# Four transposes of the probabilities ahead of the next unit's scores, in the attention of the second block's latents

## The chip, the cores and the metric

The kernel runs on one core of one Trainium2 chip. The metric is the device time of one execution in microseconds (us), as the median of several runs. Engines are named as the profile names them: PE (TensorE matmul), PEld (TensorE weight load, which overlaps PE), DVE (VectorE), ACT (ScalarE), POOL (GpSimd) and SP (the queue of transfers).

## What is computed

Two transformer blocks on 512 tokens ("latents") of width 1024. The change lies in the second block, which has two layers. Each layer has a differential attention of 8 heads, in which the 512 latents attend to 768 keys (their own 512 and 256 of a context). Cut to what matters:

```
def diff_attention(q, k, v, lam):
    s = jnp.einsum('bqahd,bkahd->bahqk', q, k).astype(jnp.float32) * (B_QK_DIM ** -0.5)
    p = jax.nn.softmax(s, axis=-1)
    a = (p[:, 0] - lam * p[:, 1]).astype(v.dtype)
    return jnp.einsum('bhqk,bkhe->bqhe', a, v)
```

Every head has two queries and two keys of 64 features (index `a`). Two softmaxes over the same 768 keys are made, the second is subtracted with a factor, and the difference weighs the values, which are 128 wide. Around it stand projections of 1024 columns and more, a spatial gate, a gated convolution, and three gated branches (`a`, `c`, `b`), each a large product.

## The kernel before

The program is a list of steps, `order`. Each engine walks the whole list and emits its own instructions of each step, so that the order of work on an engine is the order of the list, and no engine overtakes itself. A part (`DiffAttention`, `HeadNorm`, `Branch`, `Gemm`) has methods `tensor`, `scalar` and `vector` for PE, ACT and DVE. Semaphores tie the engines together.

`DiffAttention` works in units: unit u is one head and 128 of the 512 queries, 32 units in a layer. Each of its even steps, number 2t, is what I call block t on PE:

- the scores of unit t (L1592): four matmuls, of 512 and then of 256 keys for each of the two `a`, into PSUM banks 2 and 3 and banks 4 and 5. Each has 64 rows, the two `a` lie on different halves of the array, and the profile shows each of them as two matmuls, x8 in all;
- the first four transposes of unit t-1 (L1572, `turn(pe, t - 1, 0)`), four 128x128 pieces of its probabilities `p0` into bank 7;
- the product of unit t-2 with the values (L1604), 6 matmuls, x12 in the profile;
- the last two transposes of unit t-1 (`turn(pe, t - 1, 1)`), into bank 7 again.

Around it, for one unit: DVE takes the maximum of each of the two score matrices (L1649) and turns it into a bias (L1653). ACT makes the two exponentials and their sums (L1623); ahead of them it copies the first four transposes of the unit before out of bank 7, and behind them the last two (L1632, `pT`). DVE then folds the two probabilities into one, `p0` (L1660, L1662, L1665, semaphore `diff_folded`, in the code `self.pn`), and scales and clips the product of the unit two before (L1672, L1675). The scores of the next unit go to the same banks as those just folded, so that PE waits for `diff_folded` before it begins them; the transposes read `p0` and wait for the same. `turn(..., 0)` waits besides for ACT's copy of the last two transposes of the unit before that (`diff_probsT`, in the code `self.pt`), `turn(..., 1)` for that of the first four.

Between two blocks the program puts other products of PE, the filler: pieces of the branches `a` and `c` and of the convolution, made of full-width matmuls of 512 columns (L365 to L367), in portions of 12, 24 or 36. `spread_between` mixes them by their sizes, with the steps of `HeadNorm` (transposes L1718, ACT L1731 and L1736, DVE L1756). No part of that planning looks at what a block contains, and the change leaves it as it is. Weights come through a ring of five slabs (SP transfers, POOL splits them in two parts).

Of the kernel before, what the change touches and what calls it, by code (L numbers as in the profile page):

```python
# [89 lines left out]
def program(nc, rows, w, ada_in, x_in, xc_in, mem_in, cc_in, cols_in, cst_in, rel_in, onehot_in, toe_mask_in, lam_in,  # L90
            rope_in, tri_in, flip_in, sgu_in, out):
    with ExitStack() as ctx:
# [53 lines left out]
        def pb(bank, n, o=0):  # L146
            return ps[:, 512 * bank + o:512 * bank + o + n]
# [57 lines left out]
        def tile_out(tile, n, o=0):  # L205
            return pb(tile_bank[tile], n, o)
# [71 lines left out]
        class Part:  # L278
# [11 lines left out]
            def tensor(self, pe, i):  # L290
                pass
# [57 lines left out]
        def bank_ready(pe, tile):  # L349
            if tile_nth[tile]:  # L350
                pe.wait_ge(tile_free[tile_bank[tile]], tile_nth[tile])
# [1168 lines left out]
        class DiffAttention(Part):  # L1520
# [54 lines left out]
            def tensor(self, pe, i):  # L1575
                if i % 2:
                    return
                t = i // 2
                if t == 0:
                    for c in self.clear:  # L1580
                        pe.wait_ge(*c())
                if t < self.N:
                    h, b = self.units[t]
                    if b == 0:
                        for c in self.ready_kv(h):
                            pe.wait_ge(*c)
                    if t:
                        pe.wait_ge(self.pn, self.pn0 + t)
                    for n0, n1 in ((0, 512), (512, TT)):
                        for a in range(2):  # L1590
                            r = slice(HD * a, HD * a + HD)
                            mm = nc.tensor.matmul(pb(2 + 2 * a, n1 - n0, n0), self.q[r, h, b * P:(b + 1) * P],  # L1592
                                                  self.k[r, h, n0:n1], start=True, stop=True)
                            if n1 == TT:
                                mm.then_inc(self.s, 1)
                if 0 <= t - 1 < self.N:
                    self.turn(pe, t - 1, 0)
                u = t - 2
                if 0 <= u < self.N:
                    h, b = self.units[u]  # L1600
                    pe.wait_ge(self.pt, self.pt0 + 2 * u + 2)
                    bank_ready(pe, self.tile[u])
                    for b in range(TT // P):
                        mm = nc.tensor.matmul(tile_out(self.tile[u], P), self.pT[u % 2][:, b * P:(b + 1) * P],  # L1604
                                              self.v_[:, b, h * P:(h + 1) * P], start=(b == 0), stop=(b == TT // P - 1))
                    mm.then_inc(tile_done, 1)
                if 0 <= t - 1 < self.N:
                    self.turn(pe, t - 1, 1)
# [1320 lines left out]
```

## Time and profile before

| | |
|---|---|
| median of 3 runs | 3592.96 us |
| lowest and highest | 3591.21 and 3599.41 us |
| the profiled execution's own time | 3596.96 us |
| its span in the trace | 3594.1 us |
| mean granted clock of PE | 0.977 |
| scores of the latents' attention, first and last start | 1719.6 and 3046.9 us |

The profiled execution is 4.0 us above the median. The two attentions take the stretches from about 1720 to 2020 us (layer 0) and from 2758 to 3060 us (layer 1). A start in the trace is when the instruction began; a matmul's duration holds its way through the array, so that the steps from start to start tell how much of PE it takes.

### The profile page before, as it was taken

Reading aid. Unit: us, or ns where it says so; the run is one execution under the profiler, and the core shown is the slowest. Engines: PE = TensorE matmul, PEld = TensorE weight load, DVE = VectorE, ACT = ScalarE, POOL = GpSimd, SP = SyncE. Lnnn points to the kernel's source line nnn. Section 1 sums busy time; section 2 is a strip of 40 time slices with the busy share of each in tenths; the row PEclk is TensorE's granted clock in tenths of the full one; section 3 lists DMA queues with packets and bytes.
Section 4 is the critical chain, followed back from the end, with each engine's and each line's share of the span. In section 5 each row is a group of like instructions: output and inputs, shape, how many; then the busy total and the mean of one; then the engine's idle time right before and its main releaser. Section 6 shows DMA issues by size and latency. Waiting matters only on the chain. (4 is left out here: it accounts for less than half of the span.)

```text
span 3594.1 us, 50262 instructions
## 1 busy us (share of the span) xinstructions
PE 3451.7 (96%) x19738; PEld 2922.5 (81%) x19738; DVE 1489.2 (41%) x3064; ACT 1032.0 (29%) x2793; POOL 2029.4 (56%) x1216
## 2 busy tenths in 40 slices
PE   7999989999999999899999999999999999999999
PEld 6877777877789988899777788888898777888887
DVE  7833641244873221452455314441343555134320
ACT  2146443133102110342344313220232444112210
POOL 4465363654569988746433456665564342656655
PEclk9999999989999999899999999999999999999999
DMA  7533122222664433332111222322222111223222
GB/s 288 202 137 111 62 97 106 85 87 106 222 223 146 147 130 117 136 116 87 65 59 48 77 94 89 100 93 95 107 91 78 64 53 47 95 88 100 94 90 98
DMA packets 109883, 388.91 MB, mean 108 GB/s; under 512 B 12057, under 2 KB 16537, under 8 KB 108242
## 3 DMA queue, kind: packets, MB, share of 16 engines
q1 hardware_dynamic: 89280, 315.10, 25.3%
q10 hardware_dynamic: 20370, 70.61, 5.6%
q8 instruction: 158, 2.59, 0.3%
q14 instruction: 75, 0.61, 0.1%
HBM read 379.34 MB, written 6.32 MB: 107 GB/s over the span
## 5 line engine op out<-in xcount | busy, mean ns | idle before, releaser
L2726 POOL CAST whi<-raw 128x1024 fp32r<-128x1024 f32 (+1 forms) x606 | 620.8, 1024 | 1504.0 <-DMA raw<-in_w 1503.4
L2728 POOL TENSOR_TENSOR wlo<-raw,whi 128x1024 fp32r<-128x1024 f32 (+1 forms) x606 | 1423.2, 2349 | 48.5
L365 PE MATMUL ps<-hhi,whi 128*128 128x512 f32 x1688 | 670.5, 397 | 19.6 <-DVE q L1675 8.5
L367 PE MATMUL ps<-hhi,wlo 128*128 128x512 f32 x1688 | 663.1, 393 | 0.0
L366 PE MATMUL ps<-hlo,whi 128*128 128x512 f32 x1688 | 661.5, 392 | 0.0
L365 PEld LDWEIGHTS ps<-hhi,whi 128*128 128x128 f32 x1688 | 318.5, 189 | 90.0 <-DVE q L1675 9.4
L367 PEld LDWEIGHTS ps<-hhi,wlo 128*128 128x128 f32 x1688 | 318.2, 189 | 71.9
L366 PEld LDWEIGHTS ps<-hlo,whi 128*128 128x128 f32 x1688 | 318.6, 189 | 66.7
L589 PE MATMUL ps<-whi,hhi 128*128 128x256 f32 (+1 forms) x960 | 276.8, 288 | 0.0
L591 PE MATMUL ps<-whi,hlo 128*128 128x256 f32 (+1 forms) x960 | 270.7, 282 | 0.0
L590 PE MATMUL ps<-wlo,hhi 128*128 128x256 f32 (+1 forms) x960 | 270.6, 282 | 0.0
L365 PE MATMUL ps<-chi,whi 128*128 128x256 f32 x656 | 190.8, 291 | 0.1
L366 PE MATMUL ps<-clo,whi 128*128 128x256 f32 x656 | 187.8, 286 | 0.0
L367 PE MATMUL ps<-chi,wlo 128*128 128x256 f32 x656 | 187.5, 286 | 0.0
L590 PEld LDWEIGHTS ps<-wlo,hhi 128*128 128x128 f32 x960 | 184.4, 192 | 0.1
L591 PEld LDWEIGHTS ps<-whi,hlo 128*128 128x128 f32 x960 | 184.4, 192 | 0.0
L589 PEld LDWEIGHTS ps<-whi,hhi 128*128 128x128 f32 x960 | 184.0, 192 | 0.1
L1649 DVE TENSOR_REDUCE small_d<-ps 128x1 f32<-128x768 f32 x128 | 121.8, 951 | 127.5 <-PE ps L1592 127.5
L837 DVE SCALAR_TENSOR_TENSOR f_sum<-ps,cols,f_sum 128x511 f32<-128x511 f32 x88 | 65.9, 749 | 239.6 <-ACT f_sum L882 239.6
L882 ACT ACTIVATE f_sum<-ps,cols 128x512 f32<-128x512 f32 x88 | 68.4, 779 | 269.3 <-PE ps L367 259.9
L365 PE MATMUL ps<-f_hi,whi 128*128 128x512 f32 x352 | 138.3, 393 | 0.0
L366 PE MATMUL ps<-f_lo,whi 128*128 128x512 f32 x352 | 137.6, 391 | 0.0
(427 smaller groups left out, 7029.7 us busy)
## 6 DMA issues: line engine op xcount, KB each, us to landing
raw<-in_w SPq DMA_DIRECT2D x574, 512.0 KB, 3.3
ada<-in_ada ACTq DMA_DIRECT2D x96, 512.0 KB, 4.7
raw<-in_w SPq DMA_DIRECT2D x16, 384.0 KB, 3.2
att_toe<-toe_dram ACTq DMA_DIRECT2D x12, 256.0 KB, 3.3
raw<-in_w SPq DMA_DIRECT2D x16, 192.0 KB, 2.4
x<-in_x SPq DMA_DIRECT2D x4, 512.0 KB, 9.6
cond<-in_cc ACTq DMA_DIRECT2D x2, 1024.0 KB, 7.2
kc_dram<-kc ACTq DMA_DIRECT2D x2, 1024.0 KB, 4.9
```

What stands on the lines that cost most here:

```text
L365: nc.tensor.matmul(o, whi[:, buf, c], hi[:, k, 0:n], start=(k == 0), stop=False)
L366: nc.tensor.matmul(o, whi[:, buf, c], lo[:, k, 0:n], start=False, stop=False)
L367: mm = nc.tensor.matmul(o, wlo[:, buf, c], hi[:, k, 0:n], start=False, stop=(k == kt - 1))
L589: nc.tensor.matmul(o, self.hi[:, k, a], whi[:, s % RING, c], start=(k == 0), stop=False)
L590: nc.tensor.matmul(o, self.hi[:, k, a], wlo[:, s % RING, c], start=False, stop=False)
L591: mm = nc.tensor.matmul(o, self.lo[:, k, a], whi[:, s % RING, c], start=False, stop=(k == KT - 1))
L837: return nc.vector.scalar_tensor_tensor(dst[:, 1:n], src[:, 0:n - 1], w0, dst[:, 1:n], ALU.mult, ALU.add)
L882: nc.scalar.activation(self.sum(m), self.out(m), ACT.Identity, bias=cols[:, b:b + 1], scale=cols[:, w1:w1 + 1]).then_inc(self.mid, 1)
L1649: nc.vector.tensor_reduce(small[0][:, a:a + 1], pb(2 + 2 * a, TT), AX_X, ALU.max)\
L2726: nc.gpsimd.tensor_copy(whi[:, buf, 0:c], raw[:, buf, 0:c]).then_inc(slab_hi, 1)
L2728: nc.gpsimd.tensor_tensor(wlo[:, buf, 0:c], raw[:, buf, 0:c], whi[:, buf, 0:c].bitcast(F32), ALU.subtract).then_inc(slab_split, 1)
```

## The change

The wait for `diff_folded` and the first four transposes of unit t-1 stand ahead of the scores of unit t. Block 32, which has no scores, has its transposes where it had them. Nothing is added or removed but one of two waits for the same count.

```diff
                     if t:
-                        pe.wait_ge(self.pn, self.pn0 + t)
+                        self.turn(pe, t - 1, 0)
                     for n0, n1 in ((0, 512), (512, TT)):
                         for a in range(2):
 ...
                             if n1 == TT:
                                 mm.then_inc(self.s, 1)
-                if 0 <= t - 1 < self.N:
+                if t == self.N:
                     self.turn(pe, t - 1, 0)
                 u = t - 2
```

The orders of DVE, ACT, POOL and SP are the same as before. On PE, block 1 of layer 0, the first with transposes and the only one with transposes and no product (the rows above it are filler, `k`, `q` and `cst`, `diff_p` are scores and transposes; numbers behind names count tensors):

```order
 L367 MATMUL ps<-hhi,wlo 128x512
-L1592 MATMUL ps<-k_170,q_169 128x512 [waits diff_folded]
-L1592 MATMUL ps<-k_170,q_169 128x512
-L1592 MATMUL ps<-k_170,q_169 128x256 x2
 L1572 MATMUL ps<-cst,diff_p_191 128x128 [waits diff_folded]
 L1572 MATMUL ps<-cst,diff_p_191 128x128 x3
+L1592 MATMUL ps<-k_170,q_169 128x512 x2
+L1592 MATMUL ps<-k_170,q_169 128x256 x2
 L1572 MATMUL ps<-cst,diff_p_191 128x128 [waits diff_probsT]
 L1572 MATMUL ps<-cst,diff_p_191 128x128
```

The scores now stand between the first four transposes and the last two. On PE, block 3 of the same layer, one like nearly all others (`v` marks the product of unit 1 with the values):

```order
 L366 MATMUL ps<-ab_lo,whi 128x512
 L367 MATMUL ps<-ab_hi,wlo 128x512
-L1592 MATMUL ps<-k_170,q_169 128x512 [waits diff_folded]
-L1592 MATMUL ps<-k_170,q_169 128x512
-L1592 MATMUL ps<-k_170,q_169 128x256 x2
 L1572 MATMUL ps<-cst,diff_p_191 128x128 [waits diff_probsT,diff_folded]
 L1572 MATMUL ps<-cst,diff_p_191 128x128 x3
+L1592 MATMUL ps<-k_170,q_169 128x512 x2
+L1592 MATMUL ps<-k_170,q_169 128x256 x2
 L1604 MATMUL ps<-v_171,diff_p_194 128x128 [waits tile_free6,diff_probsT]
```

The transposes moved from between scores and product to ahead of the scores, and took the wait with them.

## Rows read from the trace of the kernel before

**Rows 1.** The page's part 1: busy time, share of the span, instructions

```profile
PE 3451.7 (96%) x19738; PEld 2922.5 (81%) x19738; DVE 1489.2 (41%) x3064; ACT 1032.0 (29%) x2793; POOL 2029.4 (56%) x1216
```

**Rows 2.** Waits of PE, 1715 to 2030 us: us in total, times, longest

```profile
PE ps L365 <- DVE q L1675: 4.3, 1, 4.3
```

**Rows 3.** Waits of the weight loads (PEld), the same stretch

```profile
PEld ps L1592 <- DVE diff_p L1665: 8.4, 10, 3.0
...
PEld ps L1572 <- DVE diff_p L1665: 0.4, 1, 0.4
```

**Rows 4.** Timeline of PE, block 3: start, duration, what, count

```profile
1744.58 0.39 PE L366 MATMUL ps<-ab_lo,whi 128*128 128x512 f32 x1
1744.81 0.40 PE L367 MATMUL ps<-ab_hi,wlo 128*128 128x512 f32 x1
1745.21 1.56 PE L1592 MATMUL ps<-k,q 64*128 64x512 f32 x8
1746.70 0.66 PE L1572 MATMUL ps<-cst,diff_p 128*128 128x128 f32 x4
1747.19 1.50 PE L1604 MATMUL ps<-v,diff_p 128*128 128x128 f32 x12
1748.54 0.38 PE L1572 MATMUL ps<-cst,diff_p 128*128 128x128 f32 x2
```

**Rows 5.** Timeline of DVE, blocks 2 and 3

```profile
1744.14 1.02 DVE L1665 SCALAR_TENSOR_TENSOR diff_p<-ps,small_d,diff_p 128x768 f32<-128x768 f32 x1
...
1746.85 0.96 DVE L1649 TENSOR_REDUCE small_d<-ps 128x1 f32<-128x768 f32 x1 [0.50 <-PE ps L1592]
1747.84 0.15 DVE L1653 TENSOR_SCALAR small_d<-small_d 128x1 f32<-128x1 f32 x1
...
1750.62 1.02 DVE L1665 SCALAR_TENSOR_TENSOR diff_p<-ps,small_d,diff_p 128x768 f32<-128x768 f32 x1
```

**Rows 6.** Timeline of ACT, block 3

```profile
1747.46 0.60 ACT L1632 ACTIVATE diff_p<-ps 128x512 f32<-128x512 f32 x1 [3.59 <-PE ps L1572]
1748.03 0.90 ACT L1623 ACTIVATE diff_p<-ps,small_d 128x768 f32<-128x768 f32 x1
...
1749.97 0.37 ACT L1632 ACTIVATE diff_p<-ps 128x256 f32<-128x256 f32 x1
```

**Rows 7.** Timeline of PE, filler to scores at block 2

```profile
1738.41 0.40 PE L367 MATMUL ps<-hhi,wlo 128*128 128x512 f32 x1
1738.73 0.70 PE L1592 MATMUL ps<-k,q 64*128 64x512 f32 x2
```

**Rows 8.** Timeline of PE, filler to transposes, behind the attention of layer 0

```profile
2049.04 0.39 PE L367 MATMUL ps<-hhi,wlo 128*128 128x512 f32 x1
2049.27 0.49 PE L1718 MATMUL ps<-cst,q 128*128 128x128 f32 x3
```

**Rows 9.** Timeline of PE in the context's attention: transposes, scores, product

```profile
385.49 0.44 PE L1835 MATMUL ps<-cst,c_p 128*128 128x128 f32 x2
385.86 0.70 PE L1812 MATMUL ps<-kc,qc 64*128 64x256 f32 x2
386.49 0.71 PE L1847 MATMUL ps<-vc,c_p 128*128 128x128 f32 x4
387.03 0.59 PE L1282 MATMUL ps<-att_toe,att_flip 128*128 128x512 f32 x1
```

**Rows 10.** Timeline of PE, block 1

```profile
1727.27 1.56 PE L1592 MATMUL ps<-k,q 64*128 64x512 f32 x8 [0.37 <-DVE diff_p L1665]
...
1730.11 0.44 PE L1572 MATMUL ps<-cst,diff_p 128*128 128x128 f32 x2 [0.69 <-ACT diff_p L1632]
```

**Rows 11.** Timeline of DVE, block 21, and block 30 with the filler behind it

```profile
1908.85 0.95 DVE L1649 TENSOR_REDUCE small_d<-ps 128x1 f32<-128x768 f32 x1
...
1996.50 0.70 DVE L1075 SCALAR_TENSOR_TENSOR ps<-G,ps 128x512 f32<-128x512 f32 x1 [3.19 <-PE ps L367]
```

**Rows 12.** Timeline of PE, block 26 of layer 0

```profile
1950.99 2.93 PE L1592 MATMUL ps<-k,q 64*128 64x512 f32 x8 [2.77 <-DVE diff_p L1665]
```

## The prediction

> **What bounds the kernel now.** I read the page's busy shares first. PE is busy for 96% of the span and no other engine for more than 56% [rows 1], so the time is PE's stream of instructions plus its idle time; a change of PE's order can only move the idle time and what it costs to go from one kind of matmul to the next. Then PE's waits in the attention of layer 0. The matmuls idle 4.3 us for a clipped product once [rows 2] and 0.7 us for a copy once [rows 10]. For the fold I read the weight loads' waits, since they show short ones too: 8.4 us at 10 of the 31 blocks whose scores have to wait for it [rows 3], found by going through the starts of the scores and the ends of the fold. These are blocks 1, 3, 6, 11, 13, 14, 22, 26, 29 and 30. Block 8, with 0.14 us between fold and scores, belongs to them; and block 32 (no scores, four transposes first) waits for the fold already, the one time in [rows 3]. Layer 1 has the same blocks in the same state. I call them tight, the others loose: there the fold had ended 0.5 us or more before the scores began.
>
> **The loop that binds a tight block.** Block 3: the fold of unit 2 ends at 1744.14 + 1.02 = 1745.16 and the scores start 0.05 later [rows 4, 5]. DVE idles 0.50 us for them, so nothing of its own holds the maximum up. It starts 1.64 us after the scores' start, and the fold of unit 3 ends at 1751.64: 6.43 us from the start of the scores to the end of the fold. With the 0.05 this makes a loop of 6.48 us. PE's work in the same loop, with the smallest portion of filler, is about 6.40 us. The two limits are nearly equal, and what is put between the fold and the scores lengthens the first.
>
> **What the four transposes cost there.** They take 1747.19 - 1746.70 = 0.49 us from start to start when they stand behind scores, and I take the same when they stand behind an idle PE (in both cases the first waits for its weights). Going over to 64-row scores costs more: in the context's attention two transposes and the way to the scores take 0.37 us [rows 9], against 0.22 for two at 0.11 (12 matmuls of the same size take 1.35 [rows 4]) and 0.05 that the first is late behind scores. That leaves 0.10 for the way. So the scores of a tight block start 0.05 + 0.49 + 0.10 = 0.64 us after the fold instead of 0.05: the loop becomes 7.07 us, **+0.59 us**.
>
> **Does the earlier turn shorten that loop?** This is what could pay it back: ACT copies the first four transposes just ahead of its exponentials. The copy ended at 1748.06 and the exponential started at 1748.03 [rows 6], the bias it needs was there at 1747.84 + 0.15 = 1747.99 [rows 5]. The copy cost 0.04 us, and the second exponential does not feel it: it waits for the second maximum. I put the gain at 0; at most 0.04. The new wait in front of the scores, for the copy of the last two transposes, ends at 1750.34, 1.3 us before the fold [rows 5, 6]: it costs nothing, since ACT makes that copy right behind the exponentials for which the fold waits too.
>
> **Loose blocks.** The order goes from filler, scores, transposes, product to filler, transposes, scores, product. Filler to scores takes 0.32 us [rows 7] where a step of filler takes 0.23 [rows 4], and filler to transposes takes 0.23 [rows 8]: -0.09. Transposes that don't follow scores take 0.44 and not 0.49: -0.05. The way from transposes to scores is new: +0.10. The way from scores to whatever follows is paid as before, but the product now pays for following it: four matmuls took 386.49 to 387.03 = 0.54 [rows 9], against 0.45: +0.09. Together **+0.05 us** per loose block. The bounds: without the last two terms it would be -0.14, with nothing gained at the filler +0.14. The scores start 0.45 us later against the rest of PE's stream, which has no cost where the fold had 0.5 us or more to spare.
>
> The Trainium skill ("TensorE: Matmul & The Clock Gate", Part 3, "The mechanism") says that a weight load overlaps running matmuls only if it goes to other rows of the array. Taken by its word, every full-width load would wait for the matmul ahead of it, all ways would cost the same, and 2.0 us would drop out of the sum; the trace has full-width matmuls of 128 columns 0.11 us apart with loads of 0.19 us between them, so I stay with the rows.
>
> **The sum for a layer.**
> - Blocks 3, 6, 8, 11, 13, 26, 29: the loop applies in full, 7 x 0.59 = 4.1 us. A tight block behind a loose one comes to the same: the fold is 0.45 later, the block itself takes 0.19 more behind its scores' start in the stream (0.59 in front, less 0.49, plus 0.09), and 0.05 of it is already counted.
> - Blocks 14, 30 and 32 have 0.02 to 0.24 us to spare or follow a shift that DVE's queue has partly taken up: about 0.43 each, 1.3 us.
> - Block 22: its fold is late because DVE's maxima of unit 21 came behind other work in DVE's queue (no idle time for the scores ahead of the row at 1908.85) [rows 11]. Later scores don't move it. Only the ways count: 0.2 us.
> - Block 1: unit 0 has no transposes ahead of it, so the fold isn't later. PE gets from the scores' start to the last two transposes in 1730.11 - 1727.27 = 2.84 us now, of which 0.69 is the wait for the copy [rows 10]. Then it takes 0.59 + 1.49 = 2.08, and the copy is hidden behind the scores: -0.8 us.
> - The stall of 4.3 us for the clipped product [rows 2]: DVE gets to it through a piece of filler that it waited for at 1996.50 [rows 11]. It hangs on PE's own filler, not on the scores, and stays.
> - The 20 loose blocks: 20 x 0.05 = 1.0 us.
>
> That is 4.1 + 1.3 + 0.2 - 0.8 + 1.0 = 5.8 us, and 11.6 us for both layers. Behind the attentions nothing gives it back, as PE is the bound there too. Against the profiled execution's own 3596.96 us this makes 3608.6; that execution is 4.0 us above the median, and against 3592.96 it is **3604.5 us**, 0.32% slower. A measurement can tell about 0.2%, 7.2 us, from no change, so slower means above 3600.2.
>
> **Rivals.**
> - *Only the ways count.* If the loop has slack that I don't see (the maximum can begin on the first keys' banks, DVE's queue is in truth what holds it), tight blocks cost as loose ones: 62 x 0.05, less twice 0.8, is 1.5 us: 3594.5, no change. Against it: DVE's 0.50 us of idle time for the scores [rows 5]. For it: the unit's queue is that full at some blocks, as at 21. Half of the tight blocks so gives 3599, still within 0.2%. Chance 0.17 for all that lies within.
> - *Faster.* The gain of block 1 would be that of every block: transposes that fill PE's time while ACT copies them, and ways that are cheaper behind four transposes than behind two. With -0.14 at 62 blocks and -0.8 twice it is -10.3 us: 3582.7, if tight blocks pay nothing. It decides at whether the fold or the copy is what PE waits for; the copy was the releaser once in a layer [rows 10], the fold eleven times [rows 3]. Chance 0.04.
> - *Slower by the clock.* The idle time ahead of block 26 grows from 2.77 to about 3.3 us. In layer 0 the granted clock fell there to 0.5, the 1.2 GHz level, and the scores took 2.93 us instead of 1.56 [rows 12, 4]; in layer 1 it didn't fall. Falling there too costs 1.4 us, and two more such places, with transposes then at half speed, 3 more: 3606 to 3609. Chance 0.15, within slower. The Trainium skill (same page, Part 4) has it that transposes don't count as a busy PE in the same way; they are now the first work behind each stall. Would the clock therefore fall at more tight blocks, at 1.4 us for each of 22, it would be up to 3635. In the trace transposes ran 0.11 us apart among filler at full clock; chance 0.02.
> - *The forecast*, 0.62 of the 0.79 for slower.
>
> **Range.** From 3597 (half of the loop's cost missing, or ways at -0.05) to 3610 (the clock falls in a few places more): 8 in 10. Faster 0.04, the same 0.17, slower 0.79.
>
> **What would show it.** In the trace of the changed kernel, transposes (L1572) and not scores should wait for the fold, at the same blocks; from the end of the fold to the scores' start there should be 0.64 us at tight blocks, and 7.07 us from scores to scores where it was 6.48. Filler to transposes 0.23 us, last transpose to scores 0.20. At block 1 the wait of 0.69 us for the copy should be gone. Layer 0 from its first scores to the product of its last unit should be 5.8 us longer, and so layer 1. I would be wrong if the maximum still began 1.7 us after the fold (the scores didn't come later), if the exponentials came nearer to the maxima than 0.04 us, or if a later stall of PE, the 4.3 us one above all, shrank by what the blocks lose.

## Result and profile after

The changed kernel takes 3606.96 us (median of 9 runs, 3597.92 to 3623.58) against 3593.29 us for the kernel before in the same series (9 runs). The ratio is 1.0039, with a 95% interval from 1.0025 to 1.0053: 9 to 19 us slower, 14 us in the middle. The forecast was 11.6 us. Single runs of the two kernels spread over 17 and 26 us; the profiled execution of the changed kernel took 3615.55 us, 8.6 us above the median. In the profiles a good part of the spread arises before the latents' attention begins: its first scores start at 1719.6 us in the profile before, at 1726.5 us in the one after, and between 1710.3 and 1720.0 us in the ten profiles of the experiments, though each of these profiles has the same 10066 matmuls of PE up to there. The later start goes with more time at the lower granted clock up to there: 122.9 us in the earliest, 143.4 us before, 153.6 us after, as the trace's clock records have it. So the stretches of the trace tell more than the total. Each attention is read from the start of a layer's first scores to the start of its last matmul with the values:

| stretch of the span, us | before | after |
|---|---|---|
| up to the first scores of layer 0 | 1719.6 | 1726.5 |
| attention of layer 0 | 303.7 | 309.6 |
| between | 735.0 | 735.0 |
| attention of layer 1 | 302.9 | 309.8 |
| from there to the end | 532.8 | 532.8 |

The attentions are 5.9 and 6.9 us longer, 12.8 us in all, where 5.8 was forecast for each. Nothing is given back behind them: both other stretches stay to 0.1 us. The 6.9 us ahead of them come before the first instruction that the change moved; the 14 us of the medians are near the 12.8 us of the attentions.

The waits of PE in layer 0 of the changed kernel, 1720 to 2045 us (us in total, times, longest):

```profile
PE ps L1572 <- DVE diff_p L1665: 8.1, 12, 3.2
PE ps L365 <- DVE q L1675: 4.3, 1, 4.3
```

and of its weight loads:

```profile
PEld ps L1592 <- issue: 22.1, 96, 1.4
PEld ps L1572 <- DVE diff_p L1665: 12.1, 11, 3.4
```

It is the transposes that wait for the fold now, and the matmuls themselves idle for it at 12 blocks, 8.1 us. Before, they did so at 3 blocks, over the same stretch:

```profile
PE ps L1592 <- DVE diff_p L1665: 4.4, 3, 2.8
```

The loads, which show short waits too, saw 8.4 us at 10 blocks then [rows 3] and see 12.1 us at 11 now. The 4.3 us for the clipped product stand as they were [rows 2]. The wait for the copy at block 1 [rows 10] is gone.

PE at the loose block 2 and the tight block 3 (start, duration, what, count, idle time and who ended it):

```profile
1744.52 0.40 PE L367 MATMUL ps<-hhi,wlo 128*128 128x512 f32 x1
1744.75 0.60 PE L1572 MATMUL ps<-cst,diff_p 128*128 128x128 f32 x4
1745.28 1.56 PE L1592 MATMUL ps<-k,q 64*128 64x512 f32 x8
1746.77 1.60 PE L1604 MATMUL ps<-v,diff_p 128*128 128x128 f32 x12
1748.21 0.38 PE L1572 MATMUL ps<-cst,diff_p 128*128 128x128 f32 x2
...
1751.76 0.66 PE L1572 MATMUL ps<-cst,diff_p 128*128 128x128 f32 x4 [0.40 <-DVE diff_p L1665]
1752.34 1.56 PE L1592 MATMUL ps<-k,q 64*128 64x512 f32 x8
1753.83 1.60 PE L1604 MATMUL ps<-v,diff_p 128*128 128x128 f32 x12
```

DVE there, and under it ACT:

```profile
1750.68 1.02 DVE L1665 SCALAR_TENSOR_TENSOR diff_p<-ps,small_d,diff_p 128x768 f32<-128x768 f32 x1
...
1753.97 0.96 DVE L1649 TENSOR_REDUCE small_d<-ps 128x1 f32<-128x768 f32 x1 [1.09 <-PE ps L1592]
1754.97 0.15 DVE L1653 TENSOR_SCALAR small_d<-small_d 128x1 f32<-128x1 f32 x1
...
1757.74 1.02 DVE L1665 SCALAR_TENSOR_TENSOR diff_p<-ps,small_d,diff_p 128x768 f32<-128x768 f32 x1
```

```profile
1752.51 0.60 ACT L1632 ACTIVATE diff_p<-ps 128x512 f32<-128x512 f32 x1 [2.10 <-PE ps L1572]
1755.16 0.90 ACT L1623 ACTIVATE diff_p<-ps,small_d 128x768 f32<-128x768 f32 x1 [2.05 <-DVE small_d L1653]
```

The fold ends at 1751.70, the transposes start at 1751.76 and the scores at 1752.34, 0.64 us behind the fold (0.05 before [rows 4, 5]). The maximum starts 1.63 us after the scores, as before, but DVE has idled 1.09 us for it instead of 0.50 [rows 5]. The next fold ends at 1758.76, 7.06 us after the last: before it was 6.48. ACT has its copy done at 1753.11 and then idles 2.05 us; its exponential starts at 1755.16, 0.04 us after its bias is there (1754.97 + 0.15 = 1755.12). Before, with the copy just ahead of it, that was 0.04 us too [rows 5, 6]: the copy's earlier place brought nothing.

Block 1:

```profile
1734.14 0.66 PE L1572 MATMUL ps<-cst,diff_p 128*128 128x128 f32 x4 [0.38 <-DVE diff_p L1665]
1734.73 1.56 PE L1592 MATMUL ps<-k,q 64*128 64x512 f32 x8
1736.22 0.44 PE L1572 MATMUL ps<-cst,diff_p 128*128 128x128 f32 x2
```

From the block's first matmul to the last two transposes it takes 2.08 us, where it took 2.84 [rows 10].

Block by block, by the first instruction of PE behind each block, in the two profiles: block 1 -0.75; blocks 3, 6, 11, 13 and 29 +0.58 to +0.59; block 8 +0.67; block 14 +0.45 and +0.35 (layers 0 and 1); block 22 +0.15; block 30 +0.44; block 32 +0.39; the loose ones +0.05 (a few of them, in one layer each, are 0.1 to 0.15 off that, as they are between profiles of other kernels too), but block 31 in layer 1 -0.50. Blocks 25 and 26 together are +0.90 in layer 0 and +2.25 in layer 1. The extra of layer 1 is PE's clock, which is seen in the scores of block 26 there:

```profile
3006.59 0.66 PE L1572 MATMUL ps<-cst,diff_p 128*128 128x128 f32 x4 [3.16 <-DVE diff_p L1665]
3007.17 2.93 PE L1592 MATMUL ps<-k,q 64*128 64x512 f32 x8
```

and in the granted clock of this stretch beside one just before (length; busy time of PE, PEld, DVE, ACT, POOL with counts; clock, share of the DMA engines, GB/s):

```profile
2993.00:3000.00 7.00, 7.00 (x39) 5.89 (x38) 4.77 (x10) 2.55 (x7) 3.45 (x2) 1.00 0.05 20
3006.50:3010.50 4.00, 3.91 (x14) 2.07 (x15) 2.21 (x6) 1.09 (x2) 0.51 (x1) 0.58 0.01 2
```

PE had idled 3.16 us ahead of it. The granted clock went from full (2.4 GHz) to half (1.2 GHz) for most of the 4 us, and the scores took 2.93 us as those of block 26 in layer 0 before [rows 12]. In layer 0 the clock fell at block 26 in both kernels; of the 0.90 us there, 0.26 is that the fall slows the new order a little more (from the scores of block 26 to those of 27 it is 10.82 us instead of 10.53, where an undisturbed pair of this kind gains 0.05).

The -0.50 of block 31 is the clock as well, the other way round. Behind the 4.3 us wait it fell in both kernels and both layers, but in layer 1 before it stayed low for 6.8 us, and in layer 1 after for 3.4 us. A stretch of the first and one of the second:

```profile
3036.20:3042.50 6.30, 4.38 (x10) 3.46 (x11) 1.80 (x4) 0.00 (x0) 0.00 (x0) 0.50 0.00 0
```

```profile
3058.50:3061.50 3.00, 3.00 (x8) 2.34 (x7) 0.00 (x0) 0.00 (x0) 0.00 (x0) 0.50 0.00 0
3062.00:3068.00 6.00, 6.00 (x35) 4.39 (x34) 0.74 (x1) 1.08 (x2) 0.00 (x0) 1.00 0.00 0
```

So the 6.9 us of layer 1 hold about 1.35 us more and 0.5 us less of the low clock than the 5.9 us of layer 0.

### The profile page after: what moved, and what is told of

The parts are those of the page before. It is cut to its first block and busy times, and to the rows that moved or that the text cites. A ratio compares the mean times of both kernels' runs of the same rounds, so it can differ in the third digit from the quotient of the medians.

```text
span 3613.7 us, 50248 instructions
## 1 busy us (share of the span) xinstructions
PE 3461.5 (96%) x19738; PEld 2927.3 (81%) x19738; DVE 1495.2 (41%) x3064; ACT 1030.0 (29%) x2793; POOL 2029.4 (56%) x1216
## 5 line engine op out<-in xcount | busy, mean ns | idle before, releaser
L367 PE MATMUL ps<-f_hi,wlo 128*128 128x512 f32 x352 | 138.0, 392 | 0.0
```

The source lines that it names most:

```text
L367: mm = nc.tensor.matmul(o, wlo[:, buf, c], hi[:, k, 0:n], start=False, stop=(k == kt - 1))
```

## Experiments

All runs beside runs of the kernel before on the same chip. The lengths of the two attentions are read as above, from one profile each; the kernel before has 303.7 and 302.9 us. These lengths hold the falls of the clock, and those differ from profile to profile at blocks 26 and 31 whatever the order; so below I give what a kernel costs outside these two blocks as well.

| kernel | ratio to before | 95% interval | attentions, us |
|---|---|---|---|
| the change | 1.0039 | 1.0025 to 1.0053 | 309.6, 309.8 |
| tight_only | 1.0015 | 1.0001 to 1.0029 | 308.8, 307.2 |
| loose_only | 1.0018 | 1.0007 to 1.0030 | 308.9, 306.6 |
| split_after | 1.0020 | 1.0008 to 1.0032 | 308.9, 306.5 |
| filled | 0.9986 | 0.9976 to 0.9996 | 300.2, 299.4 |
| after_filled | 1.0022 | 1.0012 to 1.0032 | 305.7, 305.8 |
| split_before | 0.9998 | 0.9986 to 1.0010 | 302.9, 303.4 |
| best | 0.9972 | 0.9963 to 0.9981 | 297.9, 297.4 |
| best31 | 0.9945 | 0.9930 to 0.9959 | 292.4, 292.4 |
| best31_again | 0.9927 | 0.9913 to 0.9941 | 292.3, 292.3 |
| best31_after | 0.9961 | 0.9949 to 0.9973 | 297.3, 297.4 |

### Which block causes the price: tight_only and loose_only

```diff
-                    if t:
+                    if t and t in (3, 6, 8, 11, 13, 14, 22, 26, 29, 30):
+                        self.turn(pe, t - 1, 0)
+                    elif t:
                         pe.wait_ge(self.pn, self.pn0 + t)
```

against the kernel before, with the transposes of the other blocks behind the scores; loose_only has `t not in (1, 3, 6, ...)` with the same numbers besides the 1. Block 1 has the old order in both.

> The new order only in blocks 3, 6, 8, 11, 13, 14, 22, 26, 29 and 30 of each layer; all others as in the kernel before. My theory: what makes a fold late is the order in the block BEFORE the one that waits (its scores come 0.45 us later), and the waiting block itself adds only what stands between fold and scores beyond what it had anyway. So blocks 3, 6, 8, 11, 13, 26 and 29 should be 0.2 us longer each, block 22 0.15 to 0.2, blocks 14 and 30 (each behind a block that has the new order) 0.45 each: 2.4 us a layer, 4.9 us in all. Rival: the price is that of the waiting block itself, since its transposes can't fill PE while it waits: then these ten blocks cost here what they cost in the changed kernel, 0.59 each, 5.2 us a layer and 10.4 us in all.

> The counterpart: the new order in all blocks but 1, 3, 6, 8, 11, 13, 14, 22, 26, 29 and 30. My theory: blocks 3, 6, 8, 11, 13, 26, 29 and 32, which have the old order (32 in both kernels) but follow blocks with the new one, are 0.40 us longer each, blocks 14, 22 and 30 stay, and the 20 loose blocks are 0.05 longer: 4.2 us a layer, 8.4 us in all. Scores should still follow the fold by 0.05 us at the waiting blocks, with 0.4 us more idle time of PE ahead of them. Rival, as in tight_only: only the ways between kinds of matmul count, 1.0 us a layer, 2 us in all.

PE and DVE around block 3 in tight_only (the scores are L1594, the fold L1667 and the maximum L1651 there):

```profile
1740.39 0.40 PE L367 MATMUL ps<-ab_hi,wlo 128*128 128x512 f32 x1
1740.79 0.66 PE L1572 MATMUL ps<-cst,diff_p 128*128 128x128 f32 x4
1741.37 1.56 PE L1594 MATMUL ps<-k,q 64*128 64x512 f32 x8
```

```profile
1739.71 1.02 DVE L1667 SCALAR_TENSOR_TENSOR diff_p<-ps,small_d,diff_p 128x768 f32<-128x768 f32 x1
```

and in loose_only:

```profile
1740.11 1.56 PE L1594 MATMUL ps<-k,q 64*128 64x512 f32 x8 [0.39 <-DVE diff_p L1667]
```

```profile
1739.04 1.02 DVE L1667 SCALAR_TENSOR_TENSOR diff_p<-ps,small_d,diff_p 128x768 f32<-128x768 f32 x1
```

In tight_only the block with the new order starts 0.40 us after the last filler, exactly as before [rows 4], with the fold ended 0.06 us earlier: its fold isn't late. Only its own longer way adds, 0.20 us over the periods of blocks 3 and 4 together (7.06 + 8.76 us from scores to scores, against 6.48 + 9.14). Blocks 14 and 30, each behind another block of the new order, pay 0.35 to 0.45; block 8 pays 0.45 and 0.27 in the two layers. In loose_only the scores follow the fold at once (1740.06 to 1740.11), but PE has idled 0.39 us: the fold is late, since the scores of block 2 were. Both the 0.39 and the 0.20 appear, each in the kernel where it was expected, and they add up to the 0.59 of the change.

The attentions as a whole don't show this by themselves: they are 9.4 us longer in tight_only, near the rival's 10.4, and 8.9 us in loose_only. In tight_only 4.8 us of the 9.4 lie at blocks 26 and 31 (1.76 and 0.89 us in layer 0, 1.79 and 0.36 in layer 1). At block 26 of layer 0, and behind the 4.3 us wait of layer 0, the clock stayed low for 6.8 us where it was 3.4 us before, and in layer 1 it fell at block 26, where it hadn't before:

```profile
1948.00:1954.50 6.50, 6.05 (x22) 4.05 (x23) 4.22 (x8) 1.91 (x4) 0.65 (x1) 0.50 0.00 0
2992.50:2995.50 3.00, 3.00 (x16) 2.35 (x13) 2.67 (x4) 1.42 (x4) 0.00 (x0) 0.50 0.01 3
```

The other blocks add 2.5 and 2.2 us a layer, where my theory has 2.2 and the rival 4.6. In loose_only they add 4.2 and 3.8 us.

The times are not against it, 5.4 and 6.5 us by the ratios against 4.9 and 8.4 expected, though their intervals are too wide to tell 4.9 from 8.4. The rival for tight_only, 10.4 us, is at the very edge of the interval (0.4 to 10.4), and the rows contradict it; that for loose_only, 2 us, is outside (2.5 to 10.8).

### Whether fold, transposes, scores and maximum are the loop: split_after and split_before

```diff
-                    nc.vector.scalar_tensor_tensor(p0, pb(4, TT), self.fold_at[t % 2], p0, ALU.mult, ALU.add)\
-                        .then_inc(self.pn, 1)
+                    for n0, n1 in ((0, 512), (512, TT)):
+                        nc.vector.scalar_tensor_tensor(p0[:, n0:n1], pb(4, n1 - n0, n0), self.fold_at[t % 2], p0[:, n0:n1],
+                                                       ALU.mult, ALU.add).then_inc(self.pn, 1)
...
-                if part == 0:
-                    pe.wait_ge(self.pn, self.pn0 + u + 1)
+                pe.wait_ge(self.pn, self.pn0 + 2 * u + part + 1)
...
                     for n0, n1 in ((0, 512), (512, TT)):
+                        if t and n0:
+                            pe.wait_ge(self.pn, self.pn0 + 2 * t)
```

> The changed kernel, with the fold on DVE made in two parts, of keys 0 to 511 and then 512 to 767, each with its own count; the first four transposes and the scores of keys 0 to 511 wait for the first part alone. If fold, transposes, scores and maximum are the loop that sets the tight blocks, they start about 0.33 us earlier (a fold of 768 takes 1.02 us, an operation of 512 of this kind 0.68): the tight loop goes from 7.07 to about 6.75 us, 3.5 us a layer, so 7 us less than the changed kernel and about 5 us more than the one before. If PE's stream or DVE's queue as a whole sets them, the second operation's fixed cost makes it the same as the changed kernel or up to 1 us a layer longer.

> The kernel before with the fold in two parts and the scores of keys 0 to 511 waiting for the first alone. The loop of fold, scores and maximum is 6.48 us there against 6.40 of PE's own work, so little is to be had: 0.08 us at each of 7 tight blocks, 0.27 at blocks 1, 22 and 26, and 0.1 lost at the wait behind block 30 through the second operation: 1.3 us a layer, 2.6 us in all. In split_after the same edit gave 0.27 at each tight block. If it gave 0.27 here too, PE's own work would be shorter than I take it for.

Block 3 of split_after, the fold on DVE (two operations, merged in the view) and PE:

```profile
1738.24 1.14 DVE L1667 SCALAR_TENSOR_TENSOR diff_p<-ps,small_d,diff_p 128x512 f32<-128x512 f32 x2
```

```profile
1739.05 0.66 PE L1571 MATMUL ps<-cst,diff_p 128*128 128x128 f32 x4
1739.63 1.56 PE L1593 MATMUL ps<-k,q 64*128 64x512 f32 x8
```

The transposes start 0.81 us after the fold begins, where it was 1.08. From scores to scores the tight blocks take 6.79 us instead of 7.06. Nothing was changed in PE's work, so the loop through the fold is what set them. By the ratios split_after is 7 us faster than the changed kernel, as expected; its attentions are 4.0 us shorter, but outside blocks 26 and 31, with the clock, they are 3.1 and 3.4 us shorter, against 3.5 expected for each. In split_before the same blocks go from 6.48 to 6.40 and stop there, with no idle time of PE ahead of the scores: that is PE's own work, the other of the two limits. The time of split_before shows no gain (0.9998). Outside blocks 26 and 31 it saves 1.6 and 1.7 us; but in its layer 1 the clock fell behind block 26, in that of the kernel before it didn't, block 31 is 0.6 us longer in both layers, and the interval goes from 5.0 us faster to 3.6 us slower. The measured time neither shows nor excludes the 2.6 us expected.

### The wait at block 26 and the clock: filled and after_filled

```diff
-            for (first, norm, second), some in zip(units, portions(filler, len(units))):
+            some_of = list(portions(filler, len(units)))
...
+            some_of[25:28] = [some_of[26], some_of[27][:1], some_of[27][1:]]
+            for (first, norm, second), some in zip(units, some_of):
```

> The kernel before, with the filler of block 26 moved to block 25, which had none, that of block 27 split between 26 and 27; nothing else. PE waits 2.77 us for the fold at block 26, because no filler stands between 25 and 26. Expected: that wait goes, block 27 gets 12 matmuls ahead of it and becomes tight (0.08 us), so 2.7 us less a layer, 5.4 us in all; and where the clock fell to half behind that wait (1.4 us, once in the trace of the kernel before), it stays at full. If the time were bound elsewhere, by the chain of units, the wait would come back at block 27 or at the 4.3 us wait behind block 30.

> The changed kernel with the filler moved as in the run filled. It says what the two edits do together: block 26 turns loose and loses its wait of 3.16 us, block 27 turns tight and pays 0.59 us. 2.7 us a layer less than the changed kernel, and 1.4 to 1.7 us more where the clock fell to half behind that wait; against the kernel before 12.8 - 5.5 = 7 us more, or 5 with the clock. If the cost of the change had to do with block 26 above all (a longer wait, then a lower clock), it would be within 2 us of the kernel before.

PE's waits in layer 0 of filled:

```profile
PE ps L365 <- DVE q L1675: 4.3, 1, 4.3
PE ps L1592 <- DVE diff_p L1665: 1.6, 2, 1.3
```

The wait of 2.8 us is gone from the list, and at block 26 the clock falls in neither layer. The kernel is 5 us faster by the ratio, as expected; its attentions are 3.5 us shorter each. After_filled costs 8 us over the kernel before against 7 expected; its attentions are 5.5 and 6.4 us longer than those of filled, 5.9 and 5.7 us outside block 31. So the price of the change is there in full when block 26 has no long wait: it isn't a matter of that block or of the clock at it.

Over the profiles the clock fell behind block 26 in 5 of 6 layers with a wait of 2.5 to 2.8 us, in both with 2.9 us, and in 3 of 4 with 3.2 us. That doesn't show the longer wait of the new order to make the fall likelier, though twelve cases are too few to exclude it. In layer 0 the profile before had had the fall, in layer 1 not, and the 1.4 us of that difference are luck.

### Better than both: best, best31

best is the kernel before with the new order in block 1 alone (`if t == 1: self.turn(pe, 0, 0)`), with the filler of filled and the fold of split_before. best31 has besides:

```diff
             some_of[25:28] = [some_of[26], some_of[27][:1], some_of[27][1:]]
+            some_of[30:32] = [some_of[30][:1], some_of[30][1:] + some_of[31]]
```

> The kernel before with three things: the new order in block 1 alone, the filler moved as in the run filled, and the fold in two parts as in split_after. By the measured steps: block 1 -0.76 us, the filler -2.75 us, and the loop of the tight blocks, 0.27 us shorter, is then below PE's own 6.40 us, so 0.08 us at each of 7 and about 0.27 at blocks 1 and 22: 4.5 us a layer, 9 us less than the kernel before. If the gains were not additive, for instance because the filler's move already used up the slack that the shorter loop gives, it would be 6.5 us.

> The run best, with the second of block 30's two portions of filler given to block 31. It looks at the 4.3 us wait behind block 30, which every kernel so far kept unchanged: PE's second portion there needs the bank that DVE frees (L1675) behind the fold of unit 30, behind the first portion's own result. Expected: that wait goes, and block 31 gets a wait for the fold instead, since the fold of unit 30 comes 9.4 us after its scores (blocks 13 and 29, with the same other work) and PE has 6.9 us of work: 2.3 us. 2 us less a layer than best, so 13 us less than the kernel before. If the bank isn't what holds it, the wait of 4.3 us appears again behind block 31.

> The same kernel as best31, for more runs: its gain over the kernel before came out larger (19 us by the ratio) than the 13 us expected. The traces say 11.3 and 10.5 us for the two attentions, 21.8 in all, since no wait is left there behind which the clock falls. Expected again: 0.994, 18 to 22 us less than the kernel before.

best: 10 us faster, where 9 was expected. PE's waits in layer 0 of best31, whole (the scores are L1595, the fold L1669):

```profile
PE ps L1595 <- DVE diff_p L1669: 2.1, 2, 1.1
PE ps L1595 <- issue: 1.2, 1, 1.2
PE ps L1722 <- ACT q L1735: 0.4, 1, 0.4
```

The 4.3 us wait for the clipped product is gone, and a wait of 1.1 us for the fold at block 31 took its place, where I had expected 2.3. The rest of the surprise is the clock: in all nine other programs with that wait of 4.3 or 4.4 us, in both layers, the granted clock fell to half behind it; in best31 it stays at full through both attentions. It is 20 us faster than the kernel before in the first series (4 runs) and 26 us in the second (6 runs, interval 21 to 31, where 18 to 22 was expected); in the traces the attentions are 11.3 and 10.5 us shorter, and the stretch between them is about 1 us longer.

### The change once more, with no long wait: best31_after

It is best31 with `if t: self.turn(pe, t - 1, 0)` in place of `if t == 1`.

> best31 with the order under study in all blocks instead of block 1 alone. If the cost of the order is the loop of fold, transposes, scores and maximum plus the ways between kinds of matmul, it appears here too, with no long wait and no fall of the clock to confuse it: the loop goes to 6.79 us, PE's own work is 6.40, so 0.39 us at blocks 3, 6, 11, 13, 27 and 29, 0.6 at block 8, 0.2 at 14, 22 and 30 each, about 0.4 at block 31, and 0.05 at the 20 others: 5 us a layer, 10 us more than best31. If the cost in the original kernel was in truth that of longer waits and the clock behind them, it would be 2 us (only the ways).

The attentions are 5.0 and 5.1 us longer than those of best31_again, 5 expected. The medians are 3581.6 and 3568.6 us, 13 us apart where 10 was expected, of 5 and 6 runs that spread over 6 and 15 us. PE's waits for the fold in layer 0:

```profile
PE ps L1571 <- DVE diff_p L1667: 2.8, 3, 1.5
```

The loop is 6.79 us at blocks 3, 6, 11, 13, 27 and 29, against 6.40 in best31. Here neither kernel's clock falls in the attentions, and the price of the order is what the sum says.

## Why the prediction was right

- *The loop.* 6.43 us from scores to fold held (6.42 in the changed kernel), and 7.07 us was forecast for the tight loop, 7.06 measured. It rested on DVE's idle time for the scores [rows 5], and split_after shows that the loop and not PE's or DVE's total work sets these blocks.
- *The ways between kinds of matmul.* 0.05 us for a loose block, 0.05 measured (block 31 apart, where the clock comes in). Term by term: filler to transposes 0.23; transposes to scores 0.53 us from first to first (0.58 at tight blocks, 0.59 forecast); 12 matmuls of the product 1.44 us behind scores instead of 1.35. The rule that I weighed and left, by which a weight load overlaps running matmuls only on other rows (the Trainium skill, "TensorE: Matmul & The Clock Gate", Part 3, "The mechanism"), would have had these terms at zero; the loose blocks measure 0.05. That sentence isn't all that the section says: its first paragraph also lets a load that goes to the background weight buffer run ahead of the matmuls, and by that no full-width load need wait. And the 2.0 us that I said would drop out are those of the loose blocks only; the 0.10 for the way to the scores in the tight loop would have gone as well. The last transpose to the scores takes 0.20 us where transposes follow each other by 0.11.
- *ACT's copy.* Put at 0, it was 0: DVE's bias and not the copy releases the exponential.
- *Block 1.* 2.84 us to 2.08, -0.76, was forecast; it measured -0.75.
- *The shift without effect.* Block 22 pays 0.15 us (0.2 forecast) and not 0.59, since its fold hangs on DVE's queue [rows 11]. The 4.3 us wait didn't move.
- *Sizes that were off.* Block 8 costs 0.67, not 0.59. Block 26 costs about 0.85 in layer 0, since the fall of the clock slows the new order by 0.26 more than the old. PE's idle time ahead of it grew to 3.16 us and not to 3.3. In layer 0, where the clock fell behind block 26 in both profiles, the attention is 5.9 us longer; 5.8 was forecast.
- *The rival of the clock.* It came true in layer 1 of the profile, at block 26, for 1.6 us, of which block 31 gave 0.5 back. That the new order brings such falls isn't shown: the clock fell behind 5 of 6 waits of 2.5 to 2.8 us and 5 of 6 of 2.9 to 3.2 us. And the price is there without any fall, in best31_after. At the other tight blocks, where transposes now follow a short wait, it never fell, which is what I had given a chance of 0.02.
- *The rival "only the ways count"*, 0.17, is refuted by the periods (7.06 us instead of 6.48) and by loose_only.

The time came out 2.5 us above the forecast, the profile's attentions 1.2 us. Of these 1.2 us about 0.85 is the clock's luck in layer 1. The interval of 9 to 19 us doesn't resolve the 2.5 us, and that the median landed so near is in part luck too.

## What to carry to other kernels

Where an engine at 96% alternates with a chain through other engines, compare two limits block by block: its own work and the chain's loop. Here 6.40 and 6.48 us at one block in three; whatever is put between the chain's last link and the engine's first answer costs its full length there, even if the engine does the same work in all, and the price shows one block later. Before reordering, look at the order's other side: the filler between the blocks. Moving four portions of it took 17.5 us off the two attentions (7.0 in filled, 10.5 from best to best31), more than the 12.8 us that the order costs.

## What the runs showed of the hardware that I had not expected

- Behind each of 18 waits of 4.3 to 4.4 us of PE the granted clock fell to half, and after 10 of 12 waits of 2.5 to 3.2 us; after waits of 1.5 us and less within the attentions never. A wait of 4.3 us thus cost more than its length: best31 lost 3.3 us of waiting against best and gained 5.5 and 5.0 us in the two layers.
- Two DVE operations of the fold, of 512 and 256 elements, took 1.14 us, where one of 768 took 1.02: the split cost 0.12 us of DVE, and PE could begin 0.27 us earlier.
